# Dense gate and up projections by one level of Strassen, in matmuls of 512 moving columns

## The reference, cut to what matters

```python
def dense_swiglu(h, w_gate, w_up, w_down):
    return (jax.nn.silu(h @ w_gate) * (h @ w_up)) @ w_down
# h: 1024 tokens x 1024; w_gate, w_up: 1024 x 2816; w_down: 2816 x 1024
```

## Time and profile before

| | us |
|---|---|
| median of three executions (3545.18 to 3548.99) | 3545.39 |
| the profiled execution, its own time | 3547.72 |
| its span, first to last instruction | 3546.1 |
| PE busy with matmuls (25,975 of them) | 3490.4 |
| DVE busy | 1897.3 |
| ACT busy | 1571.1 |
| POOL busy | 205.9 |
| bytes moved by DMA, MB | 539.79 |

### The profile page before, as it was taken

One profiled execution on the slowest core, in us unless ns is written; L12 is line 12 of the kernel. 1 busy time (PEld: TensorE's weight loads), 2 busy tenths in 40 slices (PEclk: granted clock), 3 DMA queues, 4 the chain that ended last, 5 costly groups with the idle time before them and its releaser, 6 DMA issues.

```text
span 3546.1 us, 69547 instructions
## 1 busy us (share of the span) xinstructions
PE 3490.4 (98%) x25975; PEld 3292.2 (93%) x25975; DVE 1897.3 (54%) x2865; ACT 1571.1 (44%) x2300; POOL 205.9 (6%) x212
## 2 busy tenths in 40 slices
PE   9999899999999999989999999999999999999998
PEld 8888799999999989889999999999999888898896
DVE  6455543333333555364445445446555577586774
ACT  4455433333333343354344444435454465554653
POOL 1000000000000000021101001001000020010100
PEclk9999999999999999999999999999999999999999
DMA  5111322333333322265546446446566575565654
GB/s 201 35 47 46 138 94 95 100 93 121 95 97 96 127 92 88 84 208 156 186 156 205 166 162 203 162 158 231 194 209 217 187 241 196 201 230 192 226 198 153
DMA packets 157049, 539.79 MB, mean 152 GB/s; under 512 B 23265, under 2 KB 23273, under 8 KB 156928
## 3 DMA queue, kind: packets, MB, share of 16 engines
q1 hardware_dynamic: 129584, 467.74, 39.9%
q0 software_dynamic: 23888, 64.08, 5.2%
q10 hardware_dynamic: 3456, 6.29, 0.5%
HBM read 515.54 MB, written 43.35 MB: 158 GB/s over the span
## 4 chain that ended last, share of the span: by engine, by line
PE 95%; DVE 1%; ACT 1%; issue 1%; DMA 1%; POOL 0%; SPq 0%; ACTq 0%; DVEq 0%; POOLq 0%
PE ps L327 78%; PE ps L2059 8%; PE ps L2060 4%; PE ps L696 1%; PE ps L767 1%; PE ps L779 1%; PE ps L1983 1%; PE ps L797 0%; ACT eA L836 0%; PE ps L787 0%; PE ps L1157 0%; DMA yT<-in_xT 0%; PE ps L720 0%; PE ps L1551 0%; PE ps L2013 0%
## 5 line engine op out<-in xcount | busy, mean ns | idle before, releaser
L313 DVE TENSOR_TENSOR wl<-wraw,wh 128x1024 fp32r<-128x1024 f32 x884 | 1081.7, 1224 | 1144.0 <-ACT wh L309 1140.0
L309 ACT ACTIVATE wh<-wraw 128x1024 fp32r<-128x1024 f32 x884 | 933.9, 1057 | 1080.4 <-PE ps L327 1019.4
L327 PE MATMUL ps<-ex,wh 128*128 128x256 f32 (+2 forms) x4484 | 852.0, 289 | 3.7 <-issue 1.9
L327 PE MATMUL ps<-xs,wh 128*128 128x256 f32 x5248 | 822.1, 279 | 4.4 <-DVE xs L1096 1.9
L327 PEld LDWEIGHTS ps<-xs,wh 128*128 128x128 f32 x5248 | 697.9, 188 | 15.9 <-issue 9.8
L327 PEld LDWEIGHTS ps<-ex,wh 128*128 128x128 f32 x4484 | 705.4, 188 | 4.5 <-issue 4.4
L327 PE MATMUL ps<-ex,wl 128*128 128x288 f32 (+2 forms) x2240 | 648.1, 289 | 0.0
L327 PE MATMUL ps<-xs,wl 128*128 128x256 f32 x2624 | 513.7, 277 | 0.0
L2059 PE MATMUL ps<-ex,wh 128*128 128x480 f32 x1344 | 445.2, 383 | 0.0
L327 PEld LDWEIGHTS ps<-ex,wl 128*128 128x128 f32 x2240 | 421.1, 188 | 0.0
L327 PEld LDWEIGHTS ps<-xs,wl 128*128 128x128 f32 x2624 | 397.3, 188 | 0.0
(11 more groups left out here) (354 smaller groups left out, 3934.3 us busy)
## 6 DMA issues: line engine op xcount, KB each, us to landing
wraw<-in_w_expert SPq DMA_DIRECT2D x676, 512.0 KB
wraw<-in_w_main SPq DMA_DIRECT2D x208, 512.0 KB
hT<-in_xT POOLq DMA_DIRECT2D x2, 2048.0 KB, 9.6
h_d<-hT POOLq DMA_DIRECT2D x2, 2048.0 KB, 10.3
hT<-h_d POOLq DMA_DIRECT2D x2, 2048.0 KB, 13.1
xrow_d<-rows ACTq DMA_DIRECT2D x16, 256.0 KB, 2.6
yraw<-y_d POOLq DMA_DIRECT2D x4, 768.0 KB, 7.9
tabA_d<-extA_d POOLq DMA_DIRECT2D x1, 2560.0 KB, 14.4
```

Source lines behind the costliest of these rows:

```text
L309: act.activation(wh[:, j], wraw[:, j], ACT.Copy).then_inc(hi_done, 1)
L313: dve.tensor_tensor(wl[:, j], wraw[:, j], wh[:, j].bitcast(F32), ALU.subtract).then_inc(lo_done, 1)
L327: mm = pe.matmul(out[:, s], a, b[:, s], start=first and part == 0 and c == 0, stop=last and part == 2 and d == n)
```

## The change

One level of Strassen's scheme (in Winograd's form, seven products and fifteen sums instead of eight products) for gate and up:

- The first two feature tiles are done as before, as four units, first for half 0 and then for half 1 (`std_pe`). The other 20 make ten pairs of tiles. For each pair, gate and then up is one 2 x 2 block product: the weights are split in two feature tiles by two halves of the 1,024 inputs, the activations in two halves of the inputs by two halves of the tokens. A block product (`pair_pe`, 20 of them) has seven groups of 4 products, each `wide`: 84 matmuls of 512 columns.
- The sums of activation blocks T1 to T4 are made once (`t_add_dve`, `t_high_act`, `t_low_dve`, tiles of 128 x 2,048). The sums of weight blocks are made for each block product on DVE (4 of 128 x 512), and the seven left operands are split (7 on ACT, 7 on DVE, of 128 x 512). Seven results are combined by one copy on ACT and seven sums on DVE; for up, four multiplications on DVE follow, for gate, four silus on ACT. Each weight unit is now loaded once.
- The normed activations need both halves at once: `bc` holds the seven right operands, scaled in place in `hT`. So `hT` goes to memory (`h_d`) beforehand in three stores, and comes back at the end of the pairs. The norm of half 1 is made during the four units of half 0; the one of half 0 begins one unit later than before (`KD + 2`).
- The activations of the SwiGLU no longer fit: each pair's four tiles (`ast`) are stored to memory (`act_d`), two stores of 512 KB, by POOL, and fetched back in 22 loads of 512 KB (`araw`, four slots) during the down projection, where ACT and DVE split them into `act_hl`. The down projection itself has the same 44 units, for half 0 and then half 1.
- The limits of `by_width` are read once, six loads on each engine ahead of the first item.
- At the end DVE scales both blocks of the last rows; POOL's multiplications and ACT's scaling are gone.

```diff
+        def scale_in_dve(dve, m, k):
+            if m == 0 and k == 0:
+                dve.wait_ge(h_st, 16)
+            if m == 1 and k % 4 == 0:
+                dve.wait_ge(h_st, 32 + 16 * (k // 4))
+            h = hT[:, k, of_half(m)]
+            dve.scalar_tensor_tensor(h, h, gains[:, 1, k:k + 1], acc[:], ALU.mult, ALU.mult).then_inc(d_t, 1)
...
+                if KD + 2 <= u < KD + 6:
+                    for k in (2 * (u - KD - 2), 2 * (u - KD - 2) + 1):
+                        high_in_act(act, 0, k)
...
+        SQUARES1 = {13: range(0, 4), 14: range(4, 7), 15: range(7, 8)}
...
+        ORDER = ((B11, 0), (T2, 1), (T3, 2), (T1, 3), (T4, 1), (B21, 2), (B22, 3))
...
+        def std_pe(pe):
+            for half in range(2):
+                for j in range(4):
+                    pe.wait_ge(lo_done, U_STD + j + 1)
+                    for k in range(KD):
+                        if j == 0:
+                            pe.wait_ge(d_lo, 8 * half + k + 1)
+                        v, kk = dense_slot(half, k)
+                        mm = product(pe, bank(4 * half + (0, 2, 1, 3)[j]), wtile(wh, j, k), wtile(wl, j, k), bc[:, v, 0, kk], bc[:, v, 1, kk],
+                                     k == 0, k == KD - 1, cuts=EVEN if k == 0 and j == 0 else None)
+                    mm.then_inc((std_mm, unit_used)[half], 1)
+                    if half == 0 and j == 0:
+                        sum_pe(pe, 1, 4)
...
+        def pair_pe(pe, i, par, ramp=False):
+            s = 2 * i + par
+            for idx, (v, to) in enumerate(ORDER):
+                pe.wait_ge(g_lo, 7 * s + (G0 + idx + 1))
+                if ramp and par == 0 and idx in (1, 2, 3, 4):
+                    pe.wait_ge(t_lo, H0 + idx)
+                if ramp and idx == 0:
+                    pe.wait_ge(g_mu, G0 + 2 * par + 2)
+                elif idx == 0:
+                    pe.wait_ge(g_m1, s + (H0 - 1))
+                elif idx < 4:
+                    pe.wait_ge(g_c, 7 * s + (G0 - 10 + idx))
+                else:
+                    pe.wait_ge(g_c, 7 * s + (G0 + (1, 2, 4)[idx - 4]))
+                ch, cl = part_of(wh, idx), part_of(wl, idx)
+                for k in range(KD // 2):
+                    kc = slice(k * P, k * P + P)
+                    mm = product(pe, bank(4 * par + to), ch[:, kc], cl[:, kc], bc[:, v, 0, k], bc[:, v, 1, k],
+                                 k == 0, k == KD // 2 - 1, wide=True)
+                mm.then_inc(g_mm, 1)
...
+            std_pe(pe)
+            for par in range(2):
+                pair_pe(pe, 0, par, True)
+            with pe.Fori(1, PAIRS_F) as i:
+                for par in range(2):
+                    pair_pe(pe, i, par)
+            pe.sem_inc(unit_used, U_DOWN - U_STD - 4)
...
+                            ready=(lambda u: pe.wait_ge(dn_lo, u + (H0 + PART * half + 1))) if part == 0 else None)
...
+        def pair_adds_dve(dve, i, par):
+            s = 2 * i + par
+            a, b = 2 * par, 2 * par + 1
+            a11, a21, a22 = wraw[:, a, 0:512], wraw[:, b, 0:512], wraw[:, b, 512:1024]
+            dve.wait_ge(raw[a], 16 * i + 16 * (Q_STD + 2))
+            dve.wait_ge(raw[b], 16 * i + 16 * (Q_STD + 2))
+            dve.tensor_tensor(st[:, 0], a21, a22, ALU.add).then_inc(g_add, 1)
+            dve.tensor_tensor(a21, a11, a21, ALU.subtract).then_inc(g_add, 1)
+            dve.wait_ge(g_add, 4 * s + (G0 + 1))
+            dve.tensor_tensor(st[:, 1], st[:, 0], a11, ALU.subtract).then_inc(g_add, 1)
+        def pair_add4_dve(dve, i, par):
+            a12 = wraw[:, 2 * par, 512:1024]
+            dve.tensor_tensor(a12, a12, st[:, 1], ALU.subtract).then_inc(g_add, 1)
...
+        def ramp_dve(dve):
+            rstd_dve(dve, 1)
+            for k in range(KD):
+                chunk_in_dve(dve, 1, k)
+            low_in_dve(dve, 1, KD - 1)
+            pair_adds_dve(dve, 0, 0)
+            for v in (T1, T3, T2):
+                t_add_dve(dve, v)
+            pair_lo_dve(dve, 0, 0, 0)
+            t_low_dve(dve, 0)
+            pair_lo_dve(dve, 0, 0, 1)
+            std_mul_dve(dve, 0, 0)
+            std_mul_dve(dve, 0, 1)
+            t_low_dve(dve, 1)
+            pair_lo_dve(dve, 0, 0, 2)
+            t_low_dve(dve, 2)
+            pair_lo_dve(dve, 0, 0, 3)
+            t_add_dve(dve, T4)
+            std_mul_dve(dve, 1, 0)
+            pair_lo_dve(dve, 0, 0, 4)
+            pair_lo_dve(dve, 0, 0, 5)
+            pair_add4_dve(dve, 0, 0)
+            std_mul_dve(dve, 1, 1)
+            t_low_dve(dve, 3)
+            pair_lo_dve(dve, 0, 0, 6)
...
+            def sum1():
+                dve.wait_ge(g_m1, s + (H0 + 1))
+                dve.wait_ge(g_mm, 7 * s + (G0 + 2))
+                dve.tensor_tensor(u2[:], m1[:], bank(b + 1), ALU.add).then_inc(g_c, 1)
+            def sum2():
+                dve.wait_ge(g_mm, 7 * s + (G0 + 3))
+                dve.wait_ge(g_c, 7 * s + (G0 + 1))
+                dve.tensor_tensor(u3[:], u2[:], bank(b + 2), ALU.add).then_inc(g_c, 1)
+            def mul(x, n):
+                if par == 1:
+                    dve.wait_ge(g_si, 4 * i + (G0 + 4 + n))
+                    dve.wait_ge(g_c, 7 * s + (G0 + (3, 5, 6, 7)[n - 1]))
+                    dve.tensor_tensor(ast[:, x], ast[:, x], sg[:, x], ALU.mult).then_inc(g_mu, 1)
+            def c22():
+                if par == 1:
+                    dve.wait_ge(g_st, 32 * i + (G0 + 32))
+                dve.wait_ge(g_mm, 7 * s + (G0 + 4))
+                dve.wait_ge(g_c, 7 * s + (G0 + 2))
+                dve.tensor_tensor(to[:, 3], u3[:], bank(b + 3), ALU.add).then_inc(g_c, 1)
+                dve.tensor_tensor(u2[:], u2[:], bank(b + 3), ALU.add).then_inc(g_c, 1)
+                mul(3, 1)
+            def c21():
+                dve.wait_ge(g_mm, 7 * s + (G0 + 5))
+                dve.tensor_tensor(to[:, 1], u3[:], bank(b + 1), ALU.subtract).then_inc(g_c, 1)
+                mul(1, 2)
+            def c11():
+                dve.wait_ge(g_mm, 7 * s + (G0 + 6))
+                dve.tensor_tensor(to[:, 0], m1[:], bank(b + 2), ALU.add).then_inc(g_c, 1)
+                mul(0, 3)
+            def c12():
+                dve.wait_ge(g_mm, 7 * s + (G0 + 7))
+                dve.wait_ge(g_c, 7 * s + (G0 + 4))
+                dve.tensor_tensor(to[:, 2], u2[:], bank(b + 3), ALU.add).then_inc(g_c, 1)
+                mul(2, 4)
...
+            n, p = i + par, 1 - par
+            pair_adds_dve(dve, n, p)
+            pair_lo_dve(dve, n, p, 0)
+            sum1()
+            pair_lo_dve(dve, n, p, 1)
+            sum2()
+            pair_lo_dve(dve, n, p, 2)
+            c22()
+            pair_lo_dve(dve, n, p, 3)
+            c21()
+            pair_lo_dve(dve, n, p, 4)
+            c11()
+            pair_lo_dve(dve, n, p, 5)
+            pair_add4_dve(dve, n, p)
+            c12()
+            pair_lo_dve(dve, n, p, 6)
...
+        def dense_pool(pool):
+            for n, (half, k0, k1) in enumerate(((0, 0, KD), (1, 0, 4), (1, 4, KD))):
+                pool.wait_ge(op_add, A0 + KD * half + k1)
+                pool.dma_start(h_d[:, k0:k1, of_half(half)], hT[:, k0:k1, of_half(half)]).then_inc(h_st, 16)
+                pool.wait_ge(h_st, 16 * n + 16)
...
+            pool.wait_ge(g_st, G0 + 32 * PAIRS_F)
+            for n in range(4):
+                fetch(n)
+            for half in range(2):
+                pool.wait_ge(g_mu, G0 + 4 * PAIRS_F + 3 + half)
+                store(half, PAIRS_F)
+            for n in range(4, 8):
+                fetch(n)
+            pool.wait_ge(g_mu, G0 + 4 * PAIRS_F + 4)
+            for half in range(2):
+                pool.dma_start(hT[:, :, of_half(half)], h_d[:, :, of_half(half)]).then_inc(h_in, 16)
+                pool.wait_ge(h_in, 16 * half + 48)
...
-            pool.wait_ge(f_in, 32)
-            pool.wait_ge(hg_ok, 6 * it + (6 + YS0))
-            pool.sem_inc(past, 1)
-            for half, g in ((0, fga), (1, fgb)):
-                c = slice(512 * half, 512 * half + 512)
-                pool.tensor_tensor(on[:, 1, c], hg[:, 1, c], g[:], ALU.mult).then_inc(z_gain, 1)
-            for s_, done in ((1, z_act), (0, z_dve)):
-                pool.wait_ge(done, FROM_ONCE + 1)
+            for s_ in range(2):
+                pool.wait_ge(z_norm, FROM_ONCE + s_ + 1)
...
+        def bounds_of(eng):
+            return [eng.value_load(upto[0:1, i:i + 1], min_val=0, max_val=NIT) for i in range(len(WIDTHS) + 1)]
+        def by_width(eng, bounds, item, frm=0):
 
             for i, w in enumerate(WIDTHS):
                 if i < frm:
                     continue
-                c0 = eng.value_load(upto[0:1, i:i + 1], min_val=0, max_val=NIT)
-                c1 = eng.value_load(upto[0:1, i + 1:i + 2], min_val=0, max_val=NIT)
+                c0, c1 = bounds[i:i + 2]
...
+            with sp.Fori(1, PAIRS_F) as i:
+                for c in range(2):
+                    sp.wait_ge(g_lo, 14 * i + (G0 + 7 * c - 7))
+                    for j in (2 * c, 2 * c + 1):
```

(73 more changed lines are left out.)

377 lines of the change are left out of this document (273 added, 104 removed).

## The result

| us | before | after |
|---|---|---|
| median of four executions | 3545.28 (3544.90 to 3548.99) | 3502.27 (3501.30 to 3503.19) |
| span of the profiled execution | 3546.1 | 3501.7 |
| PE busy | 3490.4 | 3447.6 |
| DVE busy | 1897.3 | 2042.6 |

The ratio is 0.9878, with a 95% interval of 0.9866 to 0.9890. The kernel became 43 us faster; the prediction said 52 (3493, range 3484 to 3508). In a later series (run e12) the same two kernels gave 3501.90 and 3543.62, ratio 0.9882 (0.9865 to 0.9898).

The account below looks back on a forecast made before the run. PE's streaming of matmuls was taken to bound the kernel. Terms -51.8 + 2.0 + 0 + 0.2 - 0.8 - 1.8 = -52.2 us took the median from 3545.4 to 3493.2, stated as 3493, range 3484 to 3508.

Parts of the forecast that it names:

- Matmuls removed and added: Gate and up: 80 units removed (436.2 us), 1,680 matmuls of 512 columns added at 228.8 ns (384.4 us): -51.8 us.
- array's own pace: Rival, pairs: 512-column matmuls stream in 213.3 ns, the excess belonging to the value projection; 26 us more gained, 3467; 4%.
- Can DVE and ACT follow: Loop of pairs: DVE needs 27.5 of 38.4 us, ACT at most 7.4 per block product; nothing added in steady state.
- rival of a bound DVE: Loop of pairs: POOL's stores slow DVE until it bounds, deciding from 1.09 us an operation; up to +182 us, 3675; 5%.
- The start of the pairs: First block product: PE waits once before group 4 for DVE's first result sum; +2.0 us, bounds 0 and 8.
- The change to down: Down projection: `hT` reloads and fetch 8 just fit before the ninth unit, 2 to 3 us spare; 0, bounds 0 and +6.
- rival of late handovers: Start of the pairs at its bound and down starved by `hT`: +7 us together likely, 3500; 15%.
- PE's slow rhythm: After the norm's sum, 256-column matmuls run slower until a cut; half 1's sum moves into the standard units: +0.2 us.
- The rival placed it elsewhere: Rival of slow rhythm in the 44 down units or the 256-column experts: about +10 to 12 us, 3504; 8%.
- Limits and end: Expert limits read once: -1.9 us for two gaps, +1.1 before the first expert; last rows' scalings by DVE alone: -1.8.

Follow-up runs that it names:

- e12: The changed kernel itself, nothing edited, run again on a third chip beside the kernel before: 3501.90 us, ratio 0.9882.
- e10: Changed kernel with operands or their order altered in groups of the pairs, and sides exchanged in two value projection passes; output wrong; 3569.31 us.
- e5: Changed kernel with every DVE and ACT operation in the pair loops on 8 of 512 columns; output wrong; pairs 391.99 us, whole 3551.15 us.
- e7: Changed kernel with groups 0 and 1, and 2 and 3, of each block product interleaved, so PE changes PSUM bank every third matmul: 3504.10 us.

## Why the prediction was right, and where it missed

Faster, and inside the range: the mechanism was the one foreseen. PE bounds, the Strassen step takes work off it, nothing else becomes the bound. The point forecast was 9 us too low; between the two profiled executions it was 7.8 (52.2 foreseen, 44.4 measured).

**Matmuls removed and added** is the step that failed in size: 7.6 of the 7.8 us. The other terms were off too, by +3.4 us (down 2.1, slow rhythm 0.9, start of the stage and end 0.4) and by -3.2 (start of the pairs 2.0, limits 1.2); that they cancel is luck. The prediction took the rate "from the value projection, the nearest work with that shape", 228.8 ns. The rate in the pairs was 233.3: 1,680 x 4.5 = 7.6 us. It was the same shape but not the same operands, and e10 shows that exchanging the two sides of that very projection gives 233.3. The kernel before had no matmul of 512 columns with stationary weights and moving activations (the widest were of 480, in turn with 240, in its last experts); an honest lower bound would have been 226.7 (two matmuls of 256 at 113.3) and an upper one 235.6 (two at 117.8), 380.9 to 395.8 us. The rival "array's own pace" named the operands' roles and guessed their sign wrongly: the roles matter, and in the pairs they cost.

The weighing of the Trainium skill's "Back-to-back issue gap" ("TensorE: Matmul & The Clock Gate") against the row was right in its choice: the estimate of 215.8 ns is 7.5% below the 233.3 measured, and wide matmuls did not become cheaper than two narrow ones at 113.3. But the page gives that formula for an isolated matmul; for a sustained stream of weight loads and matmuls, which is what runs here, the same section of the Trainium skill states about 131 ns for 512 columns. The prediction left that out. No trace here comes near it: the lowest steady rate measured is 226.7 ns.

**Can DVE and ACT follow.** Right. DVE gained 145 us of work (165 foreseen), and one of its result sums takes 0.68 us, far from the 1.09 from which the rival of a bound DVE would decide. e5 shows that this work costs PE nothing measurable (391.99 us with it and without).

**The start of the pairs.** Foreseen +2.0, measured 0. The order of operations was right; their durations were added up where starts lie 0.60 us apart for 0.69. DVE was 3.5 us earlier than reckoned, and PE 1.6 later.

**The change to down.** "It just fits" was right as a margin and too sure as a number. The two reloads took 32.1 us in one execution and 28.2 in another, where I had 24 for both. Within the bounds 0 and +6, waits between 0 and 2.2 us occurred. This is the small form of the rival of late handovers, at one of its two places.

**PE's slow rhythm.** Foreseen +0.2, measured about +1.1. That "it lasts until a cut" was misread: the second cut after the sum ended it in every case seen, and the standard units have only one behind theirs. The rival placed it elsewhere (down, experts); it stayed out of there.

**Limits and end.** The limits' two gaps went, 1.9 us as foreseen. The first expert lost 0.7 where +1.1 was foreseen, and the loads on the chain there are DVE's, not ACT's as reckoned; no run takes them away, so that these loads cost the 0.7 is argued. The end gave 1.66 of 1.8.

Open: why the combination of operands sets the rate, by their side or by their place in memory (in the kernel's order of allocation every activation tile tried lies behind the weights' tiles); and why the second cut ends the narrow slow rhythm. A layout with the tiles in another place was not tried.

## What to carry to other kernels

Take the rate of a matmul from a row with the same width and the same kind of stationary and moving operand; if there is none, the bounds are the fast and the slow rate of the nearest, and over 1,680 matmuls 4.5 ns are 7.6 us. Before making matmuls wider, look whether narrow ones run in their fast rhythm: here two of 256 columns took 226.7 ns in it and 235.6 out of it, and one of 512 between 226.7 and 233.3. On an engine that is never waiting, add up the distances of starts, not the durations; and a transfer that "just fits" between two others should be priced with its slowest landing.

## What the runs showed of the hardware

A matmul of 512 columns (granted clock 1.00, the level of 2.4 GHz) had three steady rates: 226.7, 228.8 and 233.3 ns, by which tiles its two operands come from and in one combination also by what ran before. With stationary weights and moving activations it was 233.3 ns whether the PSUM bank changed (e7), whether the moving or the stationary tile stayed the same (e10), and whether DVE and ACT worked beside it (e5). On DVE, operations of 128 x 512 with nothing to wait for started 0.60 us apart and are shown as 0.69 us long. Two matmuls of 256 columns had 226.7 and 235.6. Between the best and the worst of these lie 4% of a stage in which PE is shown as 100% busy in each case, so the busy share tells nothing of it; only the distance of starts does.
